# Eighth feature chunk (the gates of the last pool group) as seven block products, staged through DRAM

## The reference, cut to what matters

```
proj = rms_norm(x, g) @ w_in                       # 1024 x 1024 by 1024 x 4096
pool_x, pool_z, m_x, m_z = split(proj)             # 1024 features each
pooled_g = window_mean(pool_x_g, w_g) - pool_x_g   # 4 groups of 256 features, w = 2, 4, 8, 16
y_pool_g = (pooled_g @ pool_w_g) * pool_scale_g * silu(pool_z_g)
h = x + concat(y_pool, y_m) @ w_out
```

## Time and profile before

| what | value |
|---|---|
| median of 3 runs | 1152.65 us (1152.45 to 1152.68) |
| the profiled execution | 1152.89 us |
| its span, first to last instruction | 1151.1 us |
| mean granted TensorE clock | 0.998 |
| TensorE busy | 1140.1 us (99%), 6515 matmuls |
| VectorE busy | 727.4 us (63%) |
| GpSimd busy | 482.7 us (42%) |
| ScalarE busy | 386.5 us (34%) |

### The profile page before, as it was taken

One profiled execution on the slowest core, in us unless ns is written; L12 is line 12 of the kernel. 1 busy time (PEld: TensorE's weight loads), 2 busy tenths in 40 slices (PEclk: granted clock), 3 DMA queues, 4 the chain that ended last, 5 costly groups with the idle time before them and its releaser, 6 DMA issues.

```text
span 1151.1 us, 17423 instructions
## 1 busy us (share of the span) xinstructions
PE 1140.1 (99%) x6515; PEld 931.5 (81%) x6515; DVE 727.4 (63%) x1335; ACT 386.5 (34%) x758; POOL 482.7 (42%) x475
## 2 busy tenths in 40 slices
PE   9999999999999999999999999999999999999997
PEld 6888887888888887788888888889888887777786
DVE  5944545467344894467777964894698434556668
ACT  7432233222000022546574621341111134553422
POOL 2356655332223241244666765304224224455534
PEclk9999999999999999999999999999999999999999
DMA  8323343213325522101114241232111220142113
GB/s 245 120 64 121 99 146 104 90 51 114 110 67 193 209 69 97 52 24 28 47 42 161 64 175 45 102 124 74 43 50 38 66 71 1 38 149 101 44 40 138
DMA packets 84230, 104.07 MB, mean 90 GB/s; under 512 B 14258, under 2 KB 61578, under 8 KB 82995
## 3 DMA queue, kind: packets, MB, share of 16 engines
q1 hardware_dynamic: 76422, 99.21, 25.9%
q10 hardware_dynamic: 7724, 3.74, 1.2%
HBM read 80.35 MB, written 24.17 MB: 91 GB/s over the span
## 4 chain that ended last, share of the span: by engine, by line
PE 86%; POOL 8%; DMA 3%; ACT 1%; issue 1%; DVE 1%; POOLq 0%; DVEq 0%; ACTq 0%
PE bank L1064 20%; PE bank L1066 19%; PE bank L1065 19%; PE bank L1394 4%; POOL wlo L845 4%; PE bank L1369 4%; DMA wraw<-in_w_in 3%; PE wide L1385 2%; PE wide L1594 2%; PE bank L1333 1%; PE bank L1322 1%; PE bank L1310 1%; PE wide L1066 1%; PE wide L1065 1%; PE wide L1064 1%
## 5 line engine op out<-in xcount | busy, mean ns | idle before, releaser
L804 POOL CAST whi<-wraw 128x2048 fp32r<-128x2048 f32 x24 | 48.0, 1999 | 334.6 <-PE bank L1066 267.3
L1064 PE MATMUL bank<-x_hi,wlo 128*128 128x512 f32 x312 | 123.6, 396 | 0.0
L1064 PE MATMUL bank<-u_hi,wlo 128*128 128x512 f32 x308 | 120.6, 392 | 1.4 <-POOL wlo L808 1.4
L1066 PE MATMUL bank<-x_hi,whi 128*128 128x512 f32 x312 | 121.7, 390 | 0.0
L1065 PE MATMUL bank<-x_lo,whi 128*128 128x512 f32 x312 | 121.7, 390 | 0.0
L1066 PE MATMUL bank<-u_hi,whi 128*128 128x512 f32 x308 | 120.0, 390 | 0.0
L1065 PE MATMUL bank<-u_lo,whi 128*128 128x512 f32 x308 | 120.0, 390 | 0.0
L808 POOL TENSOR_TENSOR wlo<-wraw,whi 128x2048 fp32r<-128x2048 f32 x21 | 99.8, 4750 | 2.1 <-ACT whi L2908 0.5
L1064 PEld LDWEIGHTS bank<-x_hi,wlo 128*128 128x128 f32 x312 | 58.6, 188 | 16.1 <-issue 4.3
L1008 POOL TENSOR_SCALAR sp<-sp,rcx 128x384 f32<-128x384 f32 (+1 forms) x64 | 37.9, 606 | 76.4 <-DVE rcx L2392 76.3
L1064 PEld LDWEIGHTS bank<-u_hi,wlo 128*128 128x128 f32 x308 | 57.9, 188 | 14.8 <-POOL wlo L808 1.8
(11 more groups left out here) (431 smaller groups left out, 2846.4 us busy)
## 6 DMA issues: line engine op xcount, KB each, us to landing
wraw<-in_w_in SPq DMA_DIRECT2D x19, 1024.0 KB, 5.4
wraw<-in_w_out SPq DMA_DIRECT2D x12, 1024.0 KB, 5.4
wraw<-in_w_in SPq DMA_DIRECT2D x16, 512.0 KB, 4.8
xr<-in_x SPq DMA_DIRECT2D x8, 512.0 KB, 6.8
hst<-in_x SPq DMA_DIRECT2D x4, 1024.0 KB, 5.2
hpool<-hst SPq DMA_DIRECT2D x4, 1024.0 KB, 4.2
h<-hpool SPq DMA_DIRECT2D x4, 1024.0 KB, 7.0
resid<-h SPq DMA_DIRECT2D x8, 512.0 KB, 2.6
```

Source lines behind the costliest of these rows:

```text
L804: g_.tensor_copy(whi[w % 2][:, :, :], wraw[:, :, :]).then_inc(s["w_hi"], 1)
L1064: pe.matmul(ps, al, bh, start=(k == 0), stop=False)
L1066: return pe.matmul(ps, ah, bh, start=False, stop=(k == nk - 1))
```

## The change

The set `SEVEN` grows by one position, to 2 to 9, and w_in chunk 7 (pool_z 3) moves from the ordinary chunk `W_SZ3` to the fifth place of the block products. There are now eight chunks by seven products, and `W_SZ3` is gone. With eight of them the last place of the ring stands on the other side, and the first ordinary chunk behind them (`W_POOL[1]`) is position 10 instead of 9, on `whi[0]`, `wlo[0]` instead of `whi[1]`, `wlo[1]`. Its lo is now made by VectorE (`low_w`, put into the last chunk's step ahead of `low_mix(0)`). The gates of group 3 are stored to `szpool` like those of groups 1 and 2, and loaded back by a third `load_sz` behind the two loads of `hst`. `mixed(3)` waits for that load.

```diff
-    plan = [("w_in", c, "f") for c in (0, 12, 8, 9, 10, 13, 6, 5, 4, 1, 2, 3, 7)]
+    plan = [("w_in", c, "f") for c in (0, 12, 8, 9, 10, 13, 7, 6, 5, 4, 1, 2, 3)]
...
-SEVEN = range(2, 9)
+SEVEN = range(2, 10)
...
-    W_POOL, W_SZ3, W_OP, W_MX, W_MZ, W_OM, W_2 = (0, 9, 10, 11), 12, 13, 14, 16, 20, 24
+    W_POOL, W_OP, W_MX, W_MZ, W_OM, W_2 = (0, 10, 11, 12), 13, 14, 16, 20, 24
     N7, S0 = len(SEVEN), SEVEN[0]
-    BY_VECTOR = (W_MZ + 2, W_MZ + 3, W_OM, W_OM + 1)
+    BY_VECTOR = (W_POOL[1], W_MZ + 2, W_MZ + 3, W_OM, W_OM + 1)
...
-    sz_d = nc.dram_tensor("szpool", [P, 2, 2, S], F32).ap()
+    sz_d = nc.dram_tensor("szpool", [P, 3, 2, S], F32).ap()
...
-                sp_.dma_start(sz[:, :, :], sz_d[:, 2 - g, :, :]).then_inc(s["l_sz"], 16)
+                sp_.dma_start(sz[:, :, :], sz_d[:, 3 - g, :, :]).then_inc(s["l_sz"], 16)
...
             mix_weights(2)
-            wt(W_SZ3)
+            wt(W_OP)
             load_sz(2)
-            wt(W_OP)
             sp_.wait_ge(s["v_px"], 13)
             mix_weights(3)
             wt(W_OP + 1)
...
             for q in range(2):
                 load_h(0, q)
+            load_sz(3)
             wt(W_OP + 2)
...
                 mix(g - 1)
-            for i in range(4):
-                group(W_SZ3, i, u_hi, u_lo, "a_sz", 8 + i + 1)
...
+            def low_w(w):
+
+                ve.wait_ge(s["w_hi"], high_count(w))
+                ve.tensor_tensor(wlo[w % 2][:, :, :], wraw[:, :, :], whi[w % 2][:, :, :].bitcast(F32),
+                                 ALU.subtract).then_inc(s["w_lo"], 1)
+
...
-                if g in (1, 2):
+                if g:
                     ve.wait_ge(s["l_sz"], 16 * g)
                 else:
-                    ve.wait_ge(s["a_sz"], 8 + 4 * (g == 3))
+                    ve.wait_ge(s["a_sz"], 10)
...
                 if c == N7 - 1:
                     ve.wait_ge(s["g_blk"], 4 * N7)
+                    low_w(W_POOL[1])
                     low_mix(0)
                 add_up(c, 4)
                 add_up(c, 5)
...
-                if g == 3:
-                    ac.wait_ge(s["v_yr"], 12)
-                    for i in range(4):
-                        m, nh = i // 2, i % 2
-                        ps = filled(ac, "t_gemm", first[W_SZ3] + i + 1, "a_sz", 8 + i + 1)
-                        ac.activation(sz[:, m, nh * HALF:(nh + 1) * HALF], ps[:, :], ACT.Silu).then_inc(s["a_sz"], 1)
                 high_px(g, 1)
```

More of the change, by code:

```diff
@@ L377, in build @@
         early = {
-            "l_sz": ("l_h0", 32), "l_um0": ("l_h1", 16), "l_um1": ("l_h2", 16), "l_um2": ("l_h3", 16),
+            "l_sz": ("l_h0", 48), "l_um0": ("l_h1", 16), "l_um1": ("l_h2", 16), "l_um2": ("l_h3", 16),
             "o_st0": ("l_kB", 16 * (N7 - 1)), "o_st1": ("l_ln", 16 * (N7 - 1)),
@@ L1957, in _ @@
                         conv_steps(2)
[L1958 to L1962, removed]
             conv_steps(8)
```

## The result

| what | before | changed |
|---|---|---|
| median | 1152.55 us (4 runs, 1152.13 to 1152.68) | 1174.38 us (4 runs, 1171.13 to 1175.27) |
| ratio to before, 95% interval | | 1.0181 [1.0165, 1.0197] |
| the profiled execution | 1152.89 us | 1174.39 us |
| its span | 1151.1 us | 1172.6 us |
| mean granted TensorE clock | 0.998 | 0.989 |

The change makes the kernel 1.8% slower, which is 19.0 to 22.7 us by the interval. The quotient of the two medians is 1.0189. It lies a little above the ratio in the table, and inside its interval.

What follows compares the result with a forecast made beforehand. TensorE's matmul stream, busy 99% of the span, was taken as the bound; -2.72 + 7.41 + 5.7 + 6.2 + 3 = +19.6 us on the profiled 1152.89 gave 1172.5, as median 1172.2; range 1165 to 1178 us.

Steps and rivals of the forecast that it cites:

- Matmuls: Block products and removed gates chunk: 96 matmuls removed, 84 added, twelve fewer at 0.2267 us, -2.72 us.
- The first stop: End of block products: cast, `low_w`, `low_mix(0)` and adds in a row, stop 8.94 us instead of 1.53, +7.41 us.
- `mix(3)`: Ahead of `mix(3)`: TensorE waits for VectorE's `low_mix(3)`, no longer hidden by the group-3 gates, +5.7 us.
- The load of `sz`: Behind `mix(3)`: `mixed(3)` waits for `sz`, queued behind two `hst` loads, +6.2 us.
- The clock: Behind the stops: matmuls run at half clock after each long pause, +3 us.
- the matmul count decides: Block products: cast starts before they end, so matmuls and old stop are gained, 1148.4 us if later stops vanish; 3%.
- Only the first stop: End of block products only: VectorE catches up by `mix(3)` and loads are hidden, 1158.8 us; 4%.
- the clock costs nothing: Behind each gap: TensorE is at full pace with its first matmul, 1169.2 us; 12%.
- `sz` lands early: Behind `mix(3)`: mixed packets or faster 8 KB rows bring the load sooner, up to 4.7 us less, 1167.5; 13%.

Runs made afterwards that it cites:

- all-repairs kernel: Changed kernel with turned ring, VectorE reordered at the products' end and before `mix(3)`, GpSimd's second output chunk held back, `sz` loaded first: 1148.76 us, ratio 0.9964.
- The two experiments: Each against the changed kernel: `low_mix(0)` and two adds put ahead of `low_w`, 1169.45 us; ring of block places turned to `b % 8`, 1164.68 us.

## Why the prediction was right

The mechanism, the three places and their order and who ends each stop were as predicted. The sum came out at 19.6 us and the account at 21.5, and 1.9 of the difference is the clock. By its own steps:

1. **Matmuls**, -2.72 us. 6503 instead of 6515, and nothing else in the products: their last start at 215.14 against the predicted 214.78 is 0.36 us that had gathered in the unchanged work ahead of them (their first matmul starts at 62.80, before at 62.42). The all-repairs kernel bears the sign out.
2. **The first stop**, predicted 8.94 us, measured 9.05. The cast started 0.55 us after the last product's start (predicted 0.52), `low_w` took 2.29, `low_mix(0)` the short 2.35. The choice of the short value was the largest in this step (4.4 us), and the reason for it, GpSimd idle, is in the row: its next cast starts at 225.55, when VectorE is through. The two experiments split the stop: about half is the order behind `low_w`, and the cast behind the last product made it possible, by the ring's side.
3. **`mix(3)`**, predicted 5.7, measured 5.71. The prediction moved VectorE's chain as a whole behind `mix(2)`, and it kept its length.
4. **The load of `sz`**, predicted 6.2, measured 5.8. The triple took 10.4 us instead of 10.8. The low clock in `mix(3)` was hidden in this wait, as it said.
5. **The clock**, predicted 3, measured 4.9, and this is the mis-sized term. The prediction named as upper end 2.3 us for each of two restarts that lie open. They came in at 2.2 and 2.7. It took 3 of the 4.6, with no row for it, because the rows of before ended with the fall of the clock and never showed a return. That the upper end came nearer is luck too. It took its 4.6 us from an engine that stood still until the trace ended, and that this is close to the 4.7 us behind the first stop is chance: behind the third stop it was 5.6. Nor is the measured term fixed. Over the pace, the first restart cost 2.3 us in the changed kernel (2.2 net of the slower start that the kernel before had there too), and 1.7 to 2.1 behind the same stop in three kernels of the experiments. The third cost 1.5 to 2.8 in those that kept its stop.

Of the rivals, "the matmul count decides" was wrong for this kernel, and right about the mechanism: with the cast 8 us earlier the first stop nearly vanishes. But 10 us of the other two stops remained, so it needed more than the ring to turn the sign. "Only the first stop" and "the clock costs nothing" fell. "`sz` lands early" holds for 0.4 of its 4.7 us. The Trainium skill ("TensorE: Matmul & The Clock Gate", Part 1) puts the ramp at under 1% of a typical kernel and advises against fitting it to a certain number of slow matmuls. Here it is 0.4% of the span, but more than a fifth of what the change does. Its section "HAM oscillation" prices a restart at half the throttled time, by estimate 2.3 us for the 4.7 behind the first stop, which the measured 2.2 bears out.

## What to carry to other kernels

When a sequence that ends in a two-sided buffer gets one item more, ask again which side and which bank the last item stands on: the next stage's first operand may now be free only at the very end, and what was done beside the work comes behind it. When a stage of one engine is taken out because its work is now done elsewhere, list what the other engines did under its cover (here VectorE's last window and 3 MB of loads). A small load that someone soon waits for goes ahead of the bulk in its queue. And a gain of 2.7 us is lost to a single stop that is long enough to drop the clock, so each stop is priced with its restart, and moved work is priced with what runs beside it at its new place.

## What was not expected of the hardware

- **How long the clock takes varies.** In the changed kernel TensorE had stood still for about 3.3 us when the granted clock fell in the first stop, 5.3 in the second and 2.8 in the third, and at the end of the kernel before for about 2.1. It came back 4.7, 3.2 and 5.6 us after the first matmul. The first stop was the same 9.05 us in the kernels with `sz` first and with VectorE's order before `mix(3)` changed, and there the clock fell after 3.0 and 2.0 us. Stops of 2.1, 1.6, 1.4 and 0.8 us beyond the pace in the experiments left it at full, so a stop of about 2 us can go either way. One stop showed its fall only afterwards. In the kernel with VectorE's order changed at the block products, the third stop was 3.0 us long and ended at 330.87:

```profile
331.00:332.00 1.00, 1.00 (x5) 1.00 0.88 320
332.00:333.00 1.00, 1.00 (x5) 0.61 0.06 18
```

A restart with nothing to hide it cost 1.5 to 2.8 us. This also spreads the times of one kernel: of the four executions of the changed kernel, three have a mean granted clock of 0.989, and the fastest, at 1171.13 us, has 0.993.
- **A cast beside VectorE costs too.** In the kernel with VectorE's last window moved, GpSimd's cast reads one operand and took 2.88 us instead of 1.90, and VectorE's add beside it 2.83 instead of 1.26. The add ended 1.11 us after the cast, as it did behind the subtraction. The trace of before had a cast in the same case, outside the rows read from it: at 274.13, 0.09 us behind the start of VectorE's last window instruction (L1789, two SBUF operands, 1.23 us), GpSimd's cast took 2.89 us, and VectorE kept its time. In these rows the one that started second paid. No run was made to test that alone.
